# Router choice behind the logits, rows weighted before the norm's factor, and two shorter norm ends in a one-core decoder layer

## What is computed

```
x = layer_norm(ALPHA * x + m @ w_o, ln1_g, ln1_b)
scores = sigmoid(x @ w_router);  biased = scores + router_bias
# 8 groups of 8 experts: the 4 best groups by the sum of their two best, then the 8 best experts
routed = sum over the chosen experts of comb * (silu(x @ w_gate) * (x @ w_up)) @ w_down
shared = (silu(x @ ws_gate) * (x @ ws_up)) @ ws_down
y = layer_norm(ALPHA * x + routed + shared, ln2_g, ln2_b)
```

## Time and profile before

| | us |
|---|---|
| median of 3 runs (829.66 to 831.07) | 829.92 |
| the profiled execution | 829.7 |
| its span, first to last instruction | 828.0 |
| PE busy | 811.9 (98%) |
| DVE busy | 506.6 (61%) |
| ACT busy | 195.4 (24%) |
| POOL busy | 92.2 (11%) |
| TensorE clock granted, mean | 0.996 |

### The profile page before, as it was taken

How to read it: one execution, slowest core, us unless ns; L and a number is a source line. 1 busy time by engine, 2 the same in 40 slices (tenths; PEclk the granted TensorE clock), 3 DMA queues, 4 the chain that set the end, 5 groups by cost and what they waited for, 6 DMA issues and landing times.

```text
span 828.0 us, 12703 instructions
## 1 busy us (share of the span) xinstructions
PE 811.9 (98%) x4523; PEld 509.0 (61%) x4523; DVE 506.6 (61%) x1212; ACT 195.4 (24%) x300; POOL 92.2 (11%) x104
## 2 busy tenths in 40 slices
PE   9999999999999999899999999999999999999994
PEld 7876788888788888544545454444545454454452
DVE  6989899999741367545555454545545454553566
ACT  2210012111221005332222222222222323222225
POOL 1029700000010002100000000000000000000021
PEclk9999999999999999999999999999999999999998
DMA  8432344445489947699999999999999999999971
GB/s 328 154 129 101 127 144 141 148 153 116 157 341 418 394 153 284 209 397 416 421 418 420 420 421 420 419 422 419 422 419 421 420 420 421 419 420 420 418 316 52
DMA packets 50548, 262.03 MB, mean 316 GB/s; under 512 B 10504, under 2 KB 11272, under 8 KB 25296
## 3 DMA queue, kind: packets, MB, share of 16 engines
q1 hardware_dynamic: 45904, 252.88, 76.9%
q0 software_dynamic: 4608, 8.66, 2.8%
HBM read 267.10 MB, written 2.53 MB: 326 GB/s over the span
## 4 chain that ended last, share of the span: by engine, by line
PE 97%; DVE 1%; DMA 1%; ACT 1%; issue 0%; SPq 0%; ACTq 0%; DVEq 0%
PE banks L1209 35%; PE banks L1408 27%; PE banks L1448 14%; PE banks L1381 10%; PE banks L1356 3%; PE banks L1310 1%; PE banks L1224 1%; PE banks L1236 1%; PE banks L1386 1%; PE banks L1423 1%; DMA ring<-w_front 1%; PE banks L1474 0%; ACT cgb L682 0%; PE banks L1316 0%; DVE cgb L1119 0%
## 5 line engine op out<-in xcount | busy, mean ns | idle before, releaser
L1408 PE MATMUL banks<-high,low 128*64 128x512 f32 x848 | 226.1, 592 | 0.2 <-issue 0.2
L1209 PE MATMUL banks<-xT,ring 128*128 128x264 f32 x768 | 176.2, 389 | 0.4 <-DMA ring<-w_front 0.4
L1209 PEld LDWEIGHTS banks<-xT,ring 128*128 128x128 f32 x768 | 144.5, 190 | 30.5 <-issue 5.5
L1408 PEld LDWEIGHTS banks<-high,low 128*64 128x64 f32 x848 | 73.1, 137 | 145.4 <-issue 144.8
L1119 DVE TENSOR_TENSOR cgb<-cgb,banks 128x264 f32<-128x264 f32 x248 | 90.2, 425 | 51.4 <-PE banks L1381 51.4
L1164 DVE SCALAR_TENSOR_TENSOR high<-banks,sml,low 128x1024 f32<-128x1024 f32 x31 | 39.8, 1284 | 122.4 <-ACT low L670 122.4
L1381 PEld LDWEIGHTS banks<-xT,low 128*128 128x128 bf16 x744 | 70.3, 98 | 35.4 <-issue 24.3
L1381 PE MATMUL banks<-xT,low 128*128 128x264 bf16 x744 | 90.2, 276 | 0.0
L516 POOL DMA_INDIRECT low<-x_rows_dram,idx x32 | 31.9, 997 | 428.6 <-DVE idx L1064 407.8
L1408 PE MATMUL banks<-ring,low 128*64 128x512 f32 x176 | 77.4, 592 | 0.0
L1448 PE MATMUL banks<-high,mu 128*64 128x512 f32 x336 | 76.7, 598 | 0.3 <-DVE cgb L1119 0.3
(11 more groups left out here) (295 smaller groups left out, 925.4 us busy)
## 6 DMA issues: line engine op xcount, KB each, us to landing
high<-w_gu SPq DMA_DIRECT2D x108, 1024.0 KB, 23.6
high<-w_dn SPq DMA_DIRECT2D x42, 1024.0 KB, 23.4
ring<-w_front SPq DMA_DIRECT2D x78, 512.0 KB, 3.3
ring<-w_gu SPq DMA_DIRECT2D x22, 1024.0 KB, 25.1
us<-w_dn SPq DMA_DIRECT2D x11, 1024.0 KB, 23.6
bgb<-w_dn SPq DMA_DIRECT2D x6, 1024.0 KB, 21.4
xcb<-w_dn SPq DMA_DIRECT2D x5, 1024.0 KB, 21.7
xT<-x_t SPq DMA_DIRECT2D x4, 264.0 KB, 3.8
```

The costliest lines, as they stand in the source:

```text
L1209: ins = pe.matmul(psum[:, 6 + n % 2, 0:T], ring[:, n % RING, k], rhs[:, k], start=(k == 0), stop=(k == KC - 1))
L1408: ins = pe.matmul(psum[SL * j:SL * j + SL, GU_BANK, :], xg[:, k, SL * j:SL * j + SL], gu[slots[j]][:, k], start=(k == 0), stop=(k == KC - 1))
```

## The change

1. `deviation`: ACT takes the reciprocal root straight from the bank, with scale 1/D and EPS as a bias column; DVE does three operations on the bank and the root, and L982 goes. Both norms.
2. DVE and ACT weight the centered chunks with the norm's gain (`weighted`, four chunks each) before the deviation is known. TensorE turns `weighted`, not `x1`. The deviation enters later: as a scale column in ACT's copy of the rows (TensorE makes the columns from `dev` with three small products), and in DVE's scaling of the shared expert's products. The shift enters in ACT's copy to `xg`, which becomes eight pieces with a bias column in every visit, and for the shared expert through a 265th column of the tile that holds the shift.
3. DVE reads the turned scores directly behind the scaled logits. The filler before `turn_scores` goes. The eight products of `acc` move to DVE in visit 0, and its eight shifts to ACT in visit 0.
4. The last rows go in eight pieces of 128 columns. The load of `dn[7]` waits for the logits and the weighted chunks, not for `x1`.

The diff, cut to its core:

```diff
@@ tiles
-        cgb = sb("cgb", [P, KC, T])
+        cgb_wide = sb("cgb", [P, KC, T + 1])
+        cgb = cgb_wide[:, :, 0:T]
+        gates = (mu[:, 1], y_flat[:, 0:T])
+        dev = mu[:, 0]
+        LOGIT_BANK, BIAS_BANK, COLUMN_BANK = 4, 7, 7
+        DVE_WEIGHTED = 4
@@ SP
-                sp.wait_ge(x1_scaled, KC)
+                sp.wait_ge(logits_ready, 1)
+                sp.wait_ge(weighted_dve, DVE_WEIGHTED)
+                sp.wait_ge(weighted_act, KC - DVE_WEIGHTED)
                 sp.dma_start(dn[7], w_dn[6]).then_inc(dn_in[7], 16)
@@ POOL, at the start
+                pool.wait_ge(s_vec, 16)
+                pool.tensor_copy(cgb_wide[:, :, T], vec[:, V_LN + KC:V_LN + 2 * KC]).then_inc(shift_column, 1)
+                pool.memset(eps, EPS).then_inc(eps_ready, 1)
@@ ACT, squares
-                    act.wait_ge(var_ready, nth + 1)
-                    act.activation(mu[:, 1], mu[:, 0], ACT.Abs_reciprocal_sqrt).then_inc(std_ready, 1)
+                    if nth == 0:
+                        for n in range(DVE_WEIGHTED, KC):
+                            act.activation(weighted[:, n], src[:, n], ACT.Copy, scale=vec[:, V_LN + n:V_LN + n + 1]).then_inc(weighted_act, 1)
+                    act.wait_ge(eps_ready, 1)
+                    act.wait_ge(stat_out, 2 * nth + 2)
+                    act.activation(mu[:, 1], psum[:, SQUARE_BANK[nth], 0:T], ACT.Abs_reciprocal_sqrt, bias=eps, scale=1.0 / D).then_inc(std_ready, 1)
@@ ACT, router
-                for n in range(KC):
-                    act.wait_ge(x1_scaled, n + 1)
-                    act.activation(x1[:, n], x1[:, n], ACT.Identity, bias=vec[:, V_LN + KC + n:V_LN + KC + n + 1]).then_inc(x1_ready, 1)
+                act.wait_ge(columns_out, 1)
+                for c in range(TC):
+                    act.activation(dev_column[0:tok[c], c:c + 1], psum[0:tok[c], COLUMN_BANK, 256 + c:257 + c], ACT.Copy).then_inc(columns_ready, 1)
+                act.wait_ge(columns_ready, TC)
                 for c in range(TC):
                     act.wait_ge(xrow_turned, c + 1)
-                    act.activation(xrow[c][0:tok[c]], psum[...], ACT.Copy).then_inc(xrow_ready, 1)
+                    act.activation(xrow[c][0:tok[c]], psum[...], ACT.Copy, scale=dev_column[0:tok[c], c:c + 1]).then_inc(xrow_ready, 1)
@@ ACT, rows_in, silus, visit
-                    act.activation(xg.rearrange("p (b k) s -> p b (k s)", b=2), psum[:, 2:4], ACT.Copy).then_inc(xg_ready, 1)
+                    for k in range(KC):
+                        act.activation(xg[:, k], psum[:, 2 + k // 4, (k % 4) * P:(k % 4) * P + P], ACT.Identity, bias=vec[:, V_LN + KC + k:V_LN + KC + k + 1]).then_inc(xg_ready, 1)
-                    act.wait_ge(shared_gu, f + 1)
-                    act.activation(sil[:, f], psum[:, SHARED_BANKS[f], 0:T], ACT.Silu).then_inc(shared_silu, 1)
-                for n in range(KC):
-                    act.activation(acc[:, n], x1[:, n], ACT.Copy, scale=ALPHA).then_inc(acc_ready, 1)
+                    act.wait_ge(gates_scaled, f + 1)
+                    act.activation(gates[f], gates[f], ACT.Silu, bias=shared_shift[:, f:f + 1]).then_inc(shared_silu, 1)
+                    if first:        # behind rows_in of visit 0
+                        for n in range(KC):
+                            act.wait_ge(acc_scaled, n + 1)
+                            act.activation(acc[:, n], acc[:, n], ACT.Identity, bias=acc_shift[:, n:n + 1]).then_inc(acc_ready, 1)
-                        for q in range(QUARTERS):
-                            cols = slice(D // QUARTERS * q, D // QUARTERS * (q + 1))
+                        for q in range(PIECES):       # 8
+                            cols = slice(P * q, P * (q + 1))
@@ DVE, deviation and router
-                    dve.wait_ge(stat_out, 2 * nth + 2)
-                    do(dve.tensor_scalar(mu[:, 0], psum[:, SQUARE_BANK[nth], 0:T], 1.0 / D, EPS, ALU.mult, ALU.add))
-                    dve.sem_inc(var_ready, 1)
                     dve.wait_ge(std_ready, nth + 1)
-                    do(dve.scalar_tensor_tensor(mu[:, 2], mu[:, 1], -0.5, mu[:, 0], ALU.mult, ALU.mult))
-                    do(dve.tensor_tensor(mu[:, 2], mu[:, 2], mu[:, 1], ALU.mult))
+                    do(dve.scalar_tensor_tensor(mu[:, 2], psum[:, SQUARE_BANK[nth], 0:T], D * EPS, mu[:, 1], ALU.add, ALU.mult))
+                    do(dve.scalar_tensor_tensor(mu[:, 2], mu[:, 2], -0.5 / D, mu[:, 1], ALU.mult, ALU.mult))
...
+                weight_rows(0, 2)          # ahead of the last centering
+                weight_rows(2, DVE_WEIGHTED)
                 deviation(0)
...
-                for n in range(KC):
-                    dve.scalar_tensor_tensor(x1[:, n], r_[:, n], vec[:, V_LN + n:V_LN + n + 1], mu[:, 0], ALU.mult, ALU.mult).then_inc(x1_scaled, 1)
@@ DVE, behind the weights
+                dve.wait_ge(rows_stored, 16 * TC)
+                for f in range(FC):
+                    scale_shared(f, gates[f])      # a column copy, and bank * dev
+                st.settle()
+                dve.sem_inc(gates_scaled, FC)
+                for f in range(FC):
+                    scale_shared(FC + f, hT[:, f])
+                st.settle()
@@ DVE, visit 0, ahead of the hidden rows' product
+                        for n in range(KC):
+                            dve.scalar_tensor_tensor(acc[:, n], weighted[:, n], ALPHA, dev, ALU.mult, ALU.mult).then_inc(acc_scaled, 1)
+                        dve.wait_ge(acc_scaled, KC)
@@ PE, router
-                keep_warm(6, 2)
+                turn_block(0)              # eight transposes of weighted
+                pe.wait_ge(bias_ready, 1)
+                pe.wait_ge(dev_ready, 1)
+                for c in range(TC):
+                    ins = pe.matmul(psum[0:tok[c], COLUMN_BANK, 256 + c:257 + c], dev[:, c * P:c * P + tok[c]], ident[:, 0:1], start=True, stop=True)
+                ins.then_inc(columns_out, 1)
                 turn_scores()
+                turn_block(1)
...
-                for k in range(KC):
-                    pe.wait_ge(x1_ready, k + 1)
-                    for c in range(2):
-                        ins = turn_x1(c, k)
-                    shared_in(0, k, k + 1)
-                shared_in(1, 0, HC)
+                pe.wait_ge(shift_column, 1)
+                pe.wait_ge(columns_ready, TC)
+                shared_in(0, 0, KC)
                 pe.wait_ge(xrow_ready, 1)
+                turn_block(2)
+                shared_in(1, 0, HC)
@@ PE, visit and last rows
-                    pe.wait_ge(xg_ready, it + 1)
+                    if before is not None:
+                        pe.wait_ge(xg_ready, it * KC + KC)
                     for k in range(KC):
+                        if before is None:
+                            pe.wait_ge(xg_ready, k + 1)
-                    pe.wait_ge(last_rows, QUARTERS if LAST_BANKS[n] in (4, 5) else 1 + n // 2)
+                    pe.wait_ge(last_rows, PIECES if LAST_BANKS[n] in (4, 5) else n + 1)
```

More of the change, by code:

```diff
@@ L681, in _ @@
                     act.wait_ge(y_scaled, n + 1)
-                    act.activation(x1[:, n], x1[:, n], ACT.Identity, bias=vec[:, V_LN + 3 * KC + n:V_LN + 3 * KC + n + 1]).then_inc(y_ready, 1)
+                    act.activation(acc[:, n], acc[:, n], ACT.Identity, bias=vec[:, V_LN + 3 * KC + n:V_LN + 3 * KC + n + 1]).then_inc(y_ready, 1)
             @block.vector
@@ L997, in _, with weight_rows @@
                     center(0, r_, n)
+                def weight_rows(first, end):
+                    for n in range(first, end):
+                        dve.wait_ge(centered, n + 1)
+                        dve.tensor_scalar(weighted[:, n], r_[:, n], vec[:, V_LN + n:V_LN + n + 1], None, ALU.mult).then_inc(weighted_dve, 1)
+                weight_rows(0, 2)
                 dve.wait_ge(strips_done, STRIPS)
@@ L1297, in _ @@
                     for half in range(2):
-                        ins = pe.matmul(psum[E * half:E * half + E, 1, 0:1], wr[:, k], vec[:, V_LN + KC + k:V_LN + KC + k + 1], start=(k == 0), stop=(k == KC - 1))
+                        ins = pe.matmul(psum[E * half:E * half + E, BIAS_BANK, 0:1], wr[:, k], vec[:, V_LN + KC + k:V_LN + KC + k + 1], start=(k == 0), stop=(k == KC - 1))
                 ins.then_inc(bias_out, 1)
```

66 lines of the change are left out of this document (41 added, 25 removed).

## The result

The changed kernel is slower by a little: 831.48 us median of 22 runs (829.58 to 833.04), against 830.09 us of 22 runs of the kernel before. The ratio is 1.0015, with an interval of 1.0009 to 1.0021. The forecast was 828.2 us with a range up to 830.5: outside it, and on the other side. The profiled run took 831.84 us with a span of 830.1 us; the span before was 828.0, so the two traces differ by 2.1 us, 0.7 more than the medians do. The 22 runs are not alike in TensorE's clock: nine had a mean granted clock of 0.995 or less and a median of 832.17 us, eight had 0.997 or 0.998 and a median of 830.62. No run of the kernel before, here or beside the experiments, is under 0.996. The profiled run, at 0.994, is one of the nine.

What follows compares the result with a forecast made beforehand. The loop was taken to run at TensorE's pace with the DMA stream also full. Terms: -1.4 us (start -1.6, first visits +0.2), tail -0.45, last rows +0.1, sum -1.75, giving 828.2 us; range 827.0 to 830.5.

Steps and rivals of the forecast that it cites:

- the small store's landing: Router: ACT's third block of rows, 32 KB, stored to DRAM before POOL's gather; landing at 334.5 to 335.2, 0.15 us lost.
- the 4.2 us row: Router, kernel before: from SP's issue of the 32 KB store at 331.43 to POOL's gather start at 335.68.
- rival (1): Router: small store lands no sooner than 335.4 and gates the gather; loop 0.8 us earlier, sum -0.95, 829.0 us; chance 0.13.
- the forecast's first visit: Start of the expert loop: the first visit's products start 1.6 us earlier than 343.56.
- The eight pieces of the gathered rows: ACT's copy in each visit: eight pieces take 1.8 to 2.9 us, hidden by the 3.58 us down projection, cost 0.
- DVE in visit 0: First visit: DVE gets 5.4 us more work against 5.30 idle, so its product comes 0.2 us late (0 to 1.0).
- The odd tile: Shared products read 265 columns for 264, moving the tiles behind by 32 bytes; cost taken as 0.
- The root: Norm's reciprocal root straight from the bank: -0.45 us in the tail (-0.3 to -0.55), hidden in the first norm.
- The first two visits: DVE's adds of visit 1 wait for its own extra work: 0.3 to 0.6 us of stall for TensorE.
- the waits near 753 and 769: Late in the expert loop: TensorE's waits for the weight stream, about 0.5 us in each of two visits, would stay.
- the last rows in eight pieces: Tail: first product starts earlier, but chunk 5 waits for all eight pieces; +0.1 us (-0.1 to +0.4).
- The rival on the slower side: Expert loop: ACT's eight pieces outlast the down projection, TensorE waits 0.3 us in 31 visits; 836 us; chance 0.07.

Runs made afterwards that it cites:

- the filler: Nine filler products on TensorE between its last shared product and the wait for the gathered rows, added to the changed kernel: 830.33 us, ratio 1.0004.
- the queue's order: The changed kernel with the load of dn[7] issued behind the three row stores, nothing else changed: 828.46 us, ratio 0.9984.
- the kernel with the shared products ahead: The changed kernel with eight shared products moved ahead of TensorE's wait for the gathered rows: 830.91 us, ratio 1.001.

## Why the prediction was wrong

**The step that failed** is the small store's landing: "I put its landing at 334.5 to 335.2, bounds 332.8 (all 2.8 us) and 335.6 (none)." It landed at 337.0, beyond the bound called "none". The worse end was taken to be the time before, as if an earlier issue could at worst win nothing. What sets the landing is when the bytes ahead are moved, and then a tail ("drained" is the end of the last half microsecond over 200 GB/s):

```
kernel                         last store  drained  last row   gather   from the  from the
                               issued               packet     starts   drain     last packet
before                         331.43      332.0    334.32     335.68   3.7       1.36
changed                        328.99      333.0    335.64     337.00   4.0       1.36
changed, stores on ACT         329.46      333.0    334.96     336.33   3.3       1.37
changed, small block first     329.6       333.5    336.43     337.76   4.3       1.33
changed, dn[7] much later      329.45      330.5    333.59     334.96   4.5       1.37
changed, dn[7] behind stores   329.01      -        333.02     334.40   -         1.38
before, dn[7] behind stores    331.70      332.0    334.30     336.03   4.0       1.73
```

The issue moves between 329.0 and 331.7 and does not order the landings; the drain plus 3.3 to 4.5 us does. (For `dn[7]` right behind the stores the drain can't be read, as its own load runs on.) The tail has two parts. One is the last rows, which move one or two packets at a time until 2.0 to 3.1 us behind the drain, at the share of one engine in sixteen. The other is 1.33 to 1.39 us from the last packet to POOL's start in 11 of the 13 traces, and 1.6 and 1.7 in the two others. Why a few rows are left behind isn't shown. The prediction had 332.0 as the drain and the 4.2 us row beside it, and subtracted the lead of the issue from the sum of the two. By the row alone it should have said: the DMA engines are full until 332.0, the store waited 0.6 us of its 4.2 for that the earlier trace rows, so the tail is 3.7 and a landing before 335.7 was not to be had. That gives the rival (1) and its 829.0.

It was worse than that by 1.3 us: the first row moved 0.6 us later than before, and the last ones took 0.7 us longer. The first part goes with a dip in the stream, which moved 180 to 221 GB/s between 329 and 330 us, and 360 to 418 before. The bytes are the same. The rows' own data are not it: in the changed kernel one of the 264 packets had begun to move when the dip ended, and from 330.5 to 332 they went at 377 to 418 GB/s; in the kernel before they moved without a dip, at 360 to 426. It is the load's packets, of 8192 bytes, that took up to 1.4 us there for 0.31. What slows them stays open, and so does why the last rows took longer.

The prediction's aside on the Trainium skill (DMA: Bandwidth & Descriptors, Anatomy of one DMA), that a fixed 2 us would put the landing at 334, is not borne out: the shortest tail behind a drained stream is 3.3 us, and the shortest way from issue 4.2. That section times transfers that GpSimd issues, and these stores are issued by SP or ACT. What failed is the clock time to which the 2 us were added: at 332.0 rows were still to be moved, until 334.32, and behind the last one there are 1.36 us, less than the 2. Where nothing else moved, at the end of the kernel, four stores of 264 KB took 2.3 us from issue to landing (their median on the page of the changed kernel). The aside's other part, that a ring's descriptors are taken in order, stands in the section Queues, rings and completion order of the same page of the Trainium skill; the 2.6 us that the queue's order was worth agree with it.

**What was not priced** is the clock. The change moved TensorE's router work forward, so that it was done at 338.04, and the prediction did not ask what happens if the next input is late. Against the forecast's first visit (343.56 - 1.6 = 341.96) the profiled run is 3.67 us late. 1.5 of it is the clock: from the turn of the gathered rows to the first visit it took 4.75 us, and 3.23 with the filler ahead of it. The other 2.1 is the store. Two runs agree with that: the filler, which undoes the clock alone, gave 1.28 us of the first visit back (it met rows that came 0.24 later), the queue's order, which takes both away, 3.61. In the medians they gave 1.15 and 3.02. The changed kernel's own runs agree as well: 832.17 and 830.62 us, 1.55 apart, are the medians at a low and at a kept clock. As far as three digits of a mean clock can sort the runs, the kernel would have missed its forecast by 2.4 us with the clock kept too, and that is mostly the store.

**What held.** The scores at 322.38 (322.2 to 322.5 forecast) and the weights 1.54 us earlier. The eight pieces of the gathered rows, 2.17 us for 1.8 to 2.9, hidden in every visit. No table load in the loop (one, at 344.20, where the silu's had been). The visits' length: 14.41 us from a down projection to the next (355.02 and 369.43). DVE in visit 0 was not late: it had 0.25 us of idle time left, and 0.43 with `dn[7]` behind the stores, where the first visit starts as forecast, for the 0.2 late of the prediction. ACT's first term of visit 0 began 1.66 us behind the down projection's end (360.26 and 358.60) for about 2. The odd tile cost nothing: L1164 has a mean of 422 ns over 248, and it took 425 before. The root: 1.98 us for 2.38, -0.40 for -0.45 forecast. The first two visits cost nothing: DVE's last term was in at 365.14, ahead of TensorE's 365.48, where 0.3 to 0.6 us of stall was forecast. That the loop hands a shift on was right too, and cuts both ways: a loss of 2 us ahead of it arrives in full. But the waits near 753 and 769 did not stay, as it had them: 0.72 us of them came in the visit at 704.37 and 0.16 in that at 767.26, for 0.42 and 0.51 before, and the loop has its old length only because the sums are nearly equal. With `dn[7]` behind the stores, the prediction's terms come out at -1.54 ahead of the loop for -1.6, and the median at -1.7 for -1.75, so that version is near the forecast by its mechanism and not by luck.

**Only a size was off** for the last rows in eight pieces: +0.1 forecast, 7.01 for 6.75 us measured, +0.26. The direction and its reason stand: the product that waits for all pieces pays for each extra fixed part.

**The range** ended at 830.5, and the median is 831.48. With the store's landing bounded at 336 or later and a wait of TensorE priced at half clock, the other side would have had a place in it. The rival on the slower side was set on the loop's pieces (836 us), which never came near; the slower case that did come was rival (1) with its price taken too low, as it stopped at "no sooner than before".

## What to carry to other kernels

When a transfer that others wait for stands on a full queue, work out its landing from when the bytes ahead of it are moved, plus its tail behind a drained stream. Here an earlier issue won nothing by itself, and a load that nobody needed soon belonged behind it: that order was worth 3.0 us in the changed kernel, and nothing in the kernel before, where another chain ended later. When a change lets TensorE finish ahead of an input, price a late input twice: the idle time, and the work behind it at half the clock, which some executions get and others don't. Before work is moved off a place, look for what else it covered there, register loads among it.

## What the runs showed of the hardware

- POOL started 1.33 to 1.39 us behind the last data packet of the stores that it waited for, in 11 of 13 traces, with a small store (32 KB) or a big one (512 KB) last, on SP's queue or on ACT's. Behind the last half microsecond over 200 GB/s it was 3.3 to 4.5 us, because a few packets were left that moved one or two at a time. The page has 2.3 us from issue to landing for four stores of 264 KB at the quiet end of the kernel.
- Granted clock against TensorE's idle time just before: 2.85 and 2.96 us, and three waits of 0.73, 0.44 and 1.40 us with short work between, were followed by 0.50; 1.74, 1.21 (the kernel before, at 331.56) and 0.48 us were followed by 1.00. By the mean clocks of single runs, the fall comes in some executions of a kernel and not in others, with about 1.6 us between them. At 0.50 eight products of 265 columns took 3.69 us, at 1.00 they took 2.04. In the mean over the whole execution the fall is small: 0.994 for 0.996.
- Another queue for the stores brought 0.67 us of landing (1.1 like for like), another order on the one queue 2.6.
- Two loads of a number from memory into TensorE's registers took 1.46 us with the register work around them (342.48 to 343.94), in the kernel with the shared products ahead, and TensorE stood without a product for 1.40.
- Eight copies of 128x128 from PSUM with a bias column take 2.17 us, 0.26 apart with 0.38 for one; an estimate by the Trainium skill (ScalarE: Activation LUTs, What ACT_TABLE_LOAD costs) comes out at 0.294 apart, 2.4 us, a little high for this case.
- The changed kernel's stream moved 180 to 221 GB/s from 329 to 330 us, the kernel before 360 to 418, with the same bytes in all; single load packets of 8192 bytes took up to 1.4 us for 0.31. The cause is not shown.
